# Another order of turns between the chains of a hybrid mixer

## The reference, cut to what matters

```
pa, pb, pc = split_cols(rms_norm(x, mix_norm) @ w_in, GROUP_SPLITS)
y = concatenate([dsa_attention(pa), rwkv7_time_mix(pb), gated_deltanet(pc)]) @ w_out
```

## Time and profile before

| | us |
|---|---|
| median of 3 runs | 3790.31 (3785.46 to 3801.73) |
| the profiled execution | 3773.32 |
| its span | 3771.5 |
| TensorE busy | 3582.7 (95%) |
| VectorE busy | 1846.3 (49%) |
| ScalarE busy | 1320.8 (35%) |
| GpSimd busy | 257.3 (7%) |
| mean granted clock of TensorE (1 is 2.4 GHz) | 0.947 |

### The profile page before, as it was taken

The page is one execution under the profiler, slowest core; times in us unless marked ns, Lnnn a source line. Parts: engine busy times, 40 slices in busy tenths (PEclk is TensorE's granted clock), DMA queues, the critical chain, the costliest instruction groups (busy, mean ns, idle before and its releaser), DMA issues. The chain is left out here.

```text
span 3771.5 us, 41268 instructions
## 1 busy us (share of the span) xinstructions
PE 3582.7 (95%) x17088; PEld 2750.3 (73%) x17088; DVE 1846.3 (49%) x2870; ACT 1320.8 (35%) x1838; POOL 257.3 (7%) x145
## 2 busy tenths in 40 slices
PE   8999999989999999999999999999999998699995
PEld 6888576866888888885768667888657665578884
DVE  5333235865443444342357555434224333389995
ACT  3222235533321232122255324212123333277772
POOL 1000102000000000001020000000000000122222
PEclk9999999997999999999999769999999989699997
DMA  4443210001222222222100002222220111499994
GB/s 174 144 145 106 75 60 12 1 23 45 90 90 108 90 101 90 101 90 78 56 23 1 1 23 98 93 102 89 82 75 34 56 46 45 172 361 407 408 408 149
DMA packets 65690, 410.29 MB, mean 109 GB/s; under 512 B 6880, under 2 KB 11104, under 8 KB 22240
## 3 DMA queue, kind: packets, MB, share of 16 engines
q1 hardware_dynamic: 63200, 399.27, 28.6%
q0 software_dynamic: 2304, 8.39, 0.6%
HBM read 373.03 MB, written 34.60 MB: 108 GB/s over the span
## 5 line engine op out<-in xcount | busy, mean ns | idle before, releaser
L328 DVE TENSOR_TENSOR w_lo<-ring,w_hi 128x2048 fp32r<-128x2048 f32 x146 | 334.7, 2292 | 846.7 <-ACT w_hi L324 846.7
L324 ACT ACTIVATE w_hi<-ring 128x2048 fp32r<-128x2048 f32 x146 | 280.3, 1920 | 998.0 <-PE bank L444 584.5
L444 PE MATMUL bank<-x_hi,w_lo 128*128 128x512 f32 x1344 | 533.5, 397 | 0.0
L444 PE MATMUL bank<-x_hi,w_hi 128*128 128x512 f32 x1344 | 527.3, 392 | 0.0
L444 PE MATMUL bank<-x_lo,w_hi 128*128 128x512 f32 x1344 | 524.2, 390 | 0.0
L673 PE MATMUL bank<-xn,ring 128*128 128x512 f32 x768 | 338.7, 598 | 5.5 <-DVE xn L395 5.5
L444 PEld LDWEIGHTS bank<-x_lo,w_hi 128*128 128x128 f32 x1344 | 252.3, 188 | 62.2
L444 PEld LDWEIGHTS bank<-x_hi,w_lo 128*128 128x128 f32 x1344 | 252.3, 188 | 58.0
L444 PEld LDWEIGHTS bank<-x_hi,w_hi 128*128 128x128 f32 x1344 | 252.3, 188 | 54.5
L673 PEld LDWEIGHTS bank<-xn,ring 128*128 128x128 f32 x768 | 144.2, 191 | 185.5 <-issue 179.1
L488 PE MATMUL bank<-h_hi,w_hi 128*128 128x512 f32 x704 | 274.0, 389 | 0.0
(11 more groups left out here) (501 smaller groups left out, 5659.7 us busy)
## 6 DMA issues: line engine op xcount, KB each, us to landing
ring<-slots SPq DMA_DIRECT2D x238, 1024.0 KB, 4.9
arena<-slots SPq DMA_DIRECT2D x92, 1024.0 KB, 8.6
x_rows<-v_first SPq DMA_DIRECT2D x23, 512.0 KB, 6.8
xn<-x_rows SPq DMA_DIRECT2D x23, 512.0 KB, 8.1
y_rows<-xn SPq DMA_DIRECT2D x23, 512.0 KB, 8.8
x_aside<-xT SPq DMA_DIRECT2D x2, 2048.0 KB, 6.9
xT<-x_aside SPq DMA_DIRECT2D x2, 2048.0 KB, 8.2
xT<-x_t SPq DMA_DIRECT2D x2, 1024.0 KB, 10.4
```

What stands on the lines that cost most here:

```text
L324: e.activation(w_hi[:, k % 2, :], ring[:, k % RING, :], ACT.Copy).then_inc(*act.step(("hi", k)))
L328: e.tensor_tensor(w_lo[:, k % 2, :], ring[:, k % RING, :], w_hi[:, k % 2, :].bitcast(F32), ALU.subtract).then_inc(*dve.step(("slot", k)))
L444: made = e.matmul(bank[b + f][:, :], w.rearrange("p (k n) -> p k n", k=KC)[:, c, f * P:(f + 1) * P], (x_hi, x_lo)[part][:, c, :], start=c ...
```

## The change

Only the two strings change. Each chain keeps its own steps in its own order, and each string keeps its numbers of turns (26, 142, 127 and 214; 29, 113, 61 and 12). All three engines follow the new strings.

```
--- before.py
+++ after.py
@@ -33,19 +33,19 @@
 ARENA = 28000
 RWKV_ROOM = 11268
 TURNS = (
-    "p3 r p2 r2 p r p r p r2 p r7 p r3 p r p r p r6 p r2 p r6 p r p r p r s p r p r8 d r8 s r2 s r4 s "
-    "r10 d r2 s p2 d s2 d s r s p r p s3 d2 s d p d p r d s2 r s d s d r d s d s3 d2 r s3 d s d s2 d3 "
-    "s3 r d r s3 r d s3 r d r s3 d r d s3 r d s r d s5 d s2 d s2 r d s2 d2 s d s3 d s2 r2 d3 r2 d2 r "
-    "d r s d2 s2 r s d2 s r d s2 d s r s r d5 r s d s r d2 r2 s d2 r s3 d2 s r d s d s2 d2 s3 d s3 r2 "
-    "s3 d r s3 d r2 s3 d r d r s3 d r s3 d s2 r s d s4 r d s4 d2 s r s d s2 d s d r s d2 s d2 s2 r d2 "
-    "s d2 s2 d s d5 s d s2 d s3 r s r s3 r s3 r s3 r s3 r s3 r s3 r s3 r d s2 r s3 r s8 r s2 d6 s2 r "
-    "d s d3 s d2 r2 s d2 r s3 r d s r s d s r s d s r d s2 d r s2 d s2 r d s3 r s d s2 r d s3 d r s d "
-    "s2 r s d s2 d s3 d s3 d r s2 d s2 d s2 d s d2")
+    "p2 r p2 r2 p r p r2 p r p r3 p r4 p r3 p r p r3 p r4 p r2 p r s r p r2 p r2 p r p d r p r d p r "
+    "p r4 d p r d r d p r4 s r2 s r2 d r2 s r6 d r12 d s p r p r d s r s2 d s d r d s4 d r d r2 s r d "
+    "s2 d s d s d s3 d2 s6 d s3 r s3 d r s3 r d r s3 d r d r2 s3 d r s2 d s r s r s d r s2 d s2 r d "
+    "s2 d2 s d s d r s d3 s d r s d s2 d r d s2 d4 r s d2 s2 r s d4 r s d2 r s2 d2 r s d2 r d s2 r d2 "
+    "r d s r s2 r s d s3 d r s3 d s3 r d r s3 d r d s3 r s3 r s3 d r s d s2 r s4 d s2 d s2 d s3 d s2 "
+    "d2 s d s2 r s2 r s2 d s d2 s2 d3 s d2 r s3 r d s r s3 r s3 d r s3 d s3 r s3 r s3 r s3 r s3 r d "
+    "s3 d s2 r s2 r s2 d s2 d2 s2 d2 r s r d s d6 s2 d s d3 s r s d3 s2 r s2 d s3 d2 r d s r d s r d "
+    "s r d s2 d s2 r d s3 d s3 r d s3 d s3 r s3 r d r s3 r d s2 d2 s r d r s2 d2 s5")
 TURNS_2 = (
-    "p6 g p g p3 g2 p g f g p g p g p g p g2 p2 g f3 g f g f g f m4 g f m2 g m2 f3 g f3 g f3 g f3 g p "
-    "g f9 m p f2 g2 f g f g f p g f3 g f3 g f3 g2 f3 m p m g f3 g f3 p f3 p g f2 p g f m p g f2 p g "
-    "f4 g f2 g f3 g f g f2 p g f3 g f3 g f3 g2 p f3 g2 f g f g f3 g f13 g f2 g f2 p f3 g f g2 f g2 f2 "
-    "g3")
+    "p5 g p g2 p g p f g2 p g p g p g p g2 p g p g p g p g2 p g f g f g m2 f2 g f3 g p g f3 g f3 g f3 "
+    "g f g f2 p g f2 g m2 g m2 g m2 f5 g f4 g m f g f3 g f2 g f4 g f4 g f7 g f4 g f g f g p f m f p g "
+    "f4 g f2 g f3 g f3 p f2 m f p g f3 p m g f p f g2 f p f2 g f g2 f g f p f6 g f3 g f6 p f3 g2 f2 p "
+    "f3 g f g f g2 f2")
 CROSS_AT = ARENA - 2 * 4 * MEM
 NEG = -1e30
```

## The result

The changed kernel takes 3854.12 us (median of 4 runs, 3850.85 to 3857.08) against 3796.02 for the kernel before (3785.46 to 3806.25): a ratio of 1.0149, 95% interval 1.0111 to 1.0186, or 58 us more. The prediction said 3820, 3780 to 3850. The sign was right; the rise forecast (+30) was half of what was measured.

What follows compares the result with a forecast made beforehand. It took TensorE to bound the kernel (busy 3582.7 of 3771.5 us), leaving only idle time and clock to move. Terms 24 + 4 + 0 + 0 + 2 + 4 = +34, rounded to +30 on 3790: 3820 us, range 3780 to 3850.

Steps and rivals of the forecast that it cites:

- Term 1: Rotation of queries and keys (steps t1, t2, t3): fewer projections beside them leave TensorE idle; +12 us per layer, +24.
- Term 2: Top-k of block 2: ends about 1.5 us sooner, 4.3 us of TensorE work added behind; +2 us per layer, +4.
- Term 3: Top-k of block 3: bound by VectorE in both orders; 0 us (−2 to +2).
- Term 4: End of the layer's mixer: idle about 8.8 us instead of 6.6, less serial work behind; 0 (±2 us per layer).
- Term 5: Last block: memory steps apart, projections later, first split waits some 3 us; +2 us (−6 to +10).
- the rounding: Sum of the terms, +34 us, rounded down by 4 for work filling the rotation term's idle time; +30.
- Term 6: TensorE's clock: more idle at 630–660 and less work at 746–777 lean to the slow level; +4 us (−25 to +35).
- C: Rival, much slower: clock low from 630, +10 us per layer; layer 0 takes on layer 1's slow stretch, +17; 3857 us; chance 0.15.
- The rule weighed: Skill's rule that repeated TensorE waits bring half clock; by rule alone the sum would be some 40 to 60 us higher.

Runs made afterwards that it cites:

- e5: Kernel before's order in the layers up to the delta rule's cumulative sums, new order behind; last block as before: ratio 0.9984 to the kernel before.
- e6: New order in the layers up to the delta rule's cumulative sums, old order behind; last block as before: ratio 1.0056 to the kernel before.
- e7: Kernel before with only delta-rule projections 2 to 5 and the convolutions that empty their tiles moved up: ratio 1.0165 to the kernel before.
- e14: Changed kernel plus 9 unread wide matmuls per layer ahead of the waits for rotation steps t2 and t3: ratio 1.0128 to the kernel before.
- e16: Changed kernel plus 17 unread wide matmuls per layer, 9 beside the rotations and 8 in top-k waits: ratio 1.0094 to the kernel before.
- e1: New order in the layers only, the last block in its old order: ratio 1.0110 to the kernel before.
- e2: New order in the last block only, the layers in their old order: ratio 1.0030 to the kernel before.
- e3: e2 with two projections of the last block's gated linear attention put back among the doubling levels: ratio 1.0087 to the kernel before.
- e4: e2 with the last block's memory steps 2 to 7 put back behind steps 0 and 1: ratio 1.0052 to the kernel before.
- e8: e2 with the last block's projections 17 to 24 put back where the kernel before has them: ratio 1.0025 to the kernel before.
- e13: Kernel before plus 7 unread wide matmuls per layer in the top-k waits of blocks 2 and 3: ratio 0.9932 to the kernel before.
- e15: e13 plus 6 more unread wide matmuls per layer in rounds 12 and 13 of block 3's top-k: ratio 0.9913 to the kernel before.
- e10: Kernel before plus 80 unread narrow (128x64) matmuls per layer in the top-k of blocks 2 and 3: ratio 0.9956 to the kernel before.
- e9: Kernel before plus 20 unread wide (128x512) matmuls per layer in the top-k of blocks 2 and 3: ratio 0.9968 to the kernel before.

## Why the prediction was wrong, point by point

**What bounds the kernel** was read rightly: TensorE's idle time and its clock made the whole difference. Of the 58 us, 25 are idle time, where terms 1 to 5 less the rounding had 26, and 33 are slower work, where term 6 had 4. The other 6 us between 3820 and 3854 are the kernel before itself, 3790 in its first three runs and 3796 in four.

**Term 1, the bare rotation steps,** had its mechanism and its place right: line 1400 was forecast at 657.4 and began at 656.30, 11.2 us late. t2 began at 626.94 and t3 at 639.98, for 630.4 and 641. The waits for line 1967 stood where they were said to; 630–675 has 12.2 us of idle time, below the 14 that were to show it. Layer by layer the idle time of the mixer is up by 13.3 (42.4 for 29.1) and 12.6 us (42.5 for 29.9), where +12 was taken for this term; some 9 to 12 of it lie in the rotation's stretch, and 2.5 in front of the output, which term 4 had at nothing. e5, e6 and e7 show it by itself. What the chain lost on top of it is the next term's: the heads of block 0 behind it ended 19 us late, not 12, under a clock of 0.63.

**Term 2** (+2 per layer): the rounds of block 2's top-k ended 1.5 us sooner relative to their start, as worked out (+16.3 at the first, +14.9 at the last); the work moved behind them then met a slow stretch. **Term 3** (0): block 3's top-k took as long as before (+26.2 at the first round, +25.9 at the end of the mask behind the last); the wait was forecast at 7 us and is 6.38. **Term 4** (0): idle time of 8.8 us was forecast ahead of the output and 9.13 measured. But the output began at 970.49, 35.6 us late, not 14: 13 us are idle time, the rest slower work. **Term 5** (+2): the wait for the first split is 4.25 us for 3; the last block's idle time is 0.7 us less than before, and its 400 us, 27 more than before, are again the clock's.

**Term 6, the clock, is the step that failed.** It was taken as +4 us, with bounds of −25 and +35, and it measured +33: 58 us in the medians and the means, less the 25 of idle time (+59 in the two profiles). "More idle at 630–660 and less work at 746–777 lean to the slow side" had the sign. By the table of slow time two places make it up: the heads of the layers with 22 us of slow time more in each, which is some 22 us of time in all, and the last block with 19, some 10 us. (From block 2's top-k to block 3's the new order has rather less than the old one.) The size of the term was taken from the one row 646–661, where the clock of before stands at 0.83 behind 3.3 us of idle: from this I concluded that waits cost little clock. Waits of 3.35, 5.72 and 2.92 us within 27 us are another case, and 630–675 shows 0.63. The rival that I gave 0.15, C, had the first half of this: the level down from 630 to the end of term 1's stretch, +10 us per layer. That its 3857 us came within 3 of the measured 3854 is in part luck. Its second half, layer 0 taking on layer 1's 45 slow us, is no effect of the change: in this profile layer 0 has 24 (790–833 at 0.72) and layer 1 has 24 left, and in profiles of the old order that stretch has 10 to 49. The last block's part it did not have. The rule weighed there, from "TensorE: Matmul & The Clock Gate" of the Trainium skill, section "HAM oscillation — how this bites in real kernels", should have had more weight: that a kernel whose TensorE waits again and again pays half of its throttled time. Here e14 and e16 agree, with 26 and 53 us less held back once the waits are filled; the 40 to 60 us that I took by the rule alone were too many for the 33 measured. What I set against it, that the level does not come back as soon as TensorE is full, is a reason for a larger loss, not for a smaller one: in 884–933 TensorE is busy for 48.79 of 49 us at 0.50.

The range ended at 3850 for the same reason: the upper part of C was cut off, though +33 lies inside the bounds that the clock's term had. And what was read as the order's own (0.88 in layer 0 and 0.51 in layer 1 for the same work) was one draw of a clock that alone moves this kernel between 3771 and 3813 us.

**Not settled:** why e5 and e6 have 10 us less of slower work between them than the kernel before, e1 9 more and e2 8, and the changed kernel 33; and what makes the level fall in the last block at 2937, in a stretch with no wait over 0.4 us ahead of it (e3, e4 and e8 did not isolate it).

## What to carry to other kernels

Before moving a matrix product ahead because it is ready, ask which wait of another chain it covers where it stands: four projections moved up by some 30 turns left two steps of 9.6 us bare and cost 1.65% by themselves (e7). Where TensorE bounds a kernel, price a wait twice, once as idle time and once for the clock behind it: here the change cost 25 us of the one and 33 of the other, e7 53 and 18, e6 25 and 1. The first is a property of the order and can be forecast; the second scatters, and needs several profiles or many runs. The product of time and mean clock took the standard deviation from 10 us down to 2, so it shows small differences, but it is no time: a wait at half clock counts half.

## What the runs showed of the hardware

- One kernel, 105 runs: 3771 to 3813 us, with clocks from 0.935 to 0.947, and a product of time and clock of 3566 with a standard deviation of 2 us. The scatter of this kernel is its clock.
- Added work can make a kernel faster: 14 matmuls in all that nobody reads (7 per layer, some 0.9 us each) in waits of TensorE brought 0.68% (e13). 26 of them brought 0.87% (e15), which is not apart from it. Narrow ones, 128x64, did in e10 what wide ones did in e9.
- Once down, the clock stayed at 0.50 for 49 to 58 us with TensorE busy for 93% of it or more (884–933, 2247–2305 and 2937–2995 of the changed kernel).
- The same instructions in the same order ran at different clocks from run to run: layer 0's mixer at 0.92 and 0.89 (e4, e3), the last block in its old order at 0.94 and 0.87 (before, e6), with the same idle time.
